# A hybrid decoder step: mLSTM heads in 128-token chunks with a carried state, stacked high and low parts, and alternating value products

## The reference

```python
ya = attend(q, k, v)                    # softmax attention; decoding rows read a paged key/value cache
# mLSTM of one head: b = cumsum(log f), i = input gate, m_t = running maximum
w_ts  = exp(b_t - b_s + i_s - m_t)      # s <= t
num_t = sum_s (q_t . k_s) w_ts v_s + a_t C q_t      # C: the state from before the chunk
den_t = sum_s (q_t . k_s) w_ts     + a_t n . q_t
h_t   = num_t / max(|den_t|, exp(-m_t))
C_new = a_end C + sum_s ws_s v_s k_s^T              # also an output, with n and m
u = sigmoid(ga) * (ya @ w_att) + sigmoid(gm) * (ym @ w_mlstm);  y = x + gate * (u @ w_out)
```

## Time and profile before

| | us |
|---|---|
| three runs | 715.68, 719.31, 721.13 |
| median | 719.31 |
| the profiled execution | 719.64 |
| its span, first to last instruction | 717.9 |
| mean granted TensorE clock, as a share of 2.4 GHz | 0.972 |

### The profile page before, as it was taken

The page is one execution under the profiler, slowest core; times in us unless marked ns, Lnnn a source line. Parts: engine busy times, 40 slices in busy tenths (PEclk is TensorE's granted clock), DMA queues, the critical chain, the costliest instruction groups (busy, mean ns, idle before and its releaser), DMA issues.

```text
span 717.9 us, 14725 instructions
## 1 busy us (share of the span) xinstructions
PE 680.0 (95%) x5000; PEld 605.8 (84%) x5000; DVE 472.7 (66%) x483; ACT 333.5 (46%) x725; POOL 430.0 (60%) x286
## 2 busy tenths in 40 slices
PE   1899999999999799999999999999999999999996
PEld 0477788888789668999999999998999999999974
DVE  0626578898989974995697686775384358433435
ACT  5546746456381336464464534632422225333643
POOL 4203565485686318698679688771775556666510
PEclk9889999999999889999999999999999999999999
DMA  8968459888898868377867667766776355833202
GB/s 316 345 201 266 148 160 281 250 264 271 238 295 251 264 208 246 105 235 212 232 207 228 186 189 229 231 208 170 187 193 179 93 178 148 266 89 93 83 30 89
DMA packets 156904, 144.72 MB, mean 202 GB/s; under 512 B 7547, under 2 KB 115152, under 8 KB 156852
## 3 DMA queue, kind: packets, MB, share of 16 engines
q1 hardware_dynamic: 142984, 137.15, 63.5%
q10 hardware_dynamic: 13876, 7.02, 3.2%
HBM read 135.10 MB, written 9.11 MB: 201 GB/s over the span
## 4 chain that ended last, share of the span: by engine, by line
PE 63%; issue 10%; POOL 10%; DVE 5%; SPq 5%; DMA 4%; ACT 2%; ACTq 0%; POOLq 0%; DVEq 0%
PE ps L554 46%; POOL sb_arenaA L1553 4%; POOL sb_wL L1509 4%; PE ps L984 3%; PE ps L814 2%; DMA sb_arenaA<-in_w_ada 2%; PE ps L586 1%; POOL sb_arenaA L1587 1%; SPq L395 1%; PE ps L924 1%; DVE sb_arenaB L1973 1%; PE ps L775 1%; DVE sb_arenaA L1968 1%; SPq L396 1%; PE ps L569 1%
## 5 line engine op out<-in xcount | busy, mean ns | idle before, releaser
L1509 POOL TENSOR_TENSOR sb_wL<-sb_wraw,sb_wH 128x512 fp32r<-128x512 f32 (+1 forms) x168 | 216.3, 1304 | 191.1 <-ACT sb_wH L1014 175.0
L554 PE MATMUL ps<-sb_hH,sb_wH 128*128 128x260 f32 x1152 | 241.9, 292 | 3.7 <-POOL sb_wL L1509 3.7
L554 PE MATMUL ps<-sb_hH,sb_wL 128*128 128x260 f32 x1152 | 235.1, 286 | 0.0
L554 PE MATMUL ps<-sb_hL,sb_wH 128*128 128x260 f32 x1152 | 234.8, 286 | 0.0
L554 PEld LDWEIGHTS ps<-sb_hH,sb_wH 128*128 128x128 f32 x1152 | 181.6, 193 | 19.1 <-issue 13.6
L1014 ACT ACTIVATE sb_wH<-sb_wraw 128x512 fp32r<-128x512 f32 (+1 forms) x168 | 99.2, 612 | 188.0 <-PE ps L554 145.4
L554 PEld LDWEIGHTS ps<-sb_hL,sb_wH 128*128 128x128 f32 x1152 | 181.2, 192 | 0.0
L554 PEld LDWEIGHTS ps<-sb_hH,sb_wL 128*128 128x128 f32 x1152 | 180.8, 192 | 0.0
L1587 POOL TENSOR_TENSOR sb_arenaA<-sb_arenaA 128x2048 f32<-128x2048 f32 x28 | 101.6, 3630 | 1.5 <-DMA sb_arenaA<-in_cache_v 1.5
L1553 POOL TENSOR_TENSOR sb_arenaA<-sb_arenaA 128x1024 f32<-128x1024 f32 x22 | 59.9, 2745 | 33.6 <-DMA sb_arenaA<-in_cache_k 33.6
L1829 DVE TENSOR_REDUCE sb_arenaA<-sb_arenaA 128x2048 f32 (+1 forms) x32 | 72.9, 2284 | 3.6 <-DVE sb_arenaA L1825 2.0
(11 more groups left out here) (385 smaller groups left out, 952.3 us busy)
## 6 DMA issues: line engine op xcount, KB each, us to landing
sb_wraw<-in_w_in SPq DMA_DIRECT2D x64, 512.0 KB, 5.3
sb_arenaA<-in_cache_k SPq DMA_DIRECT2D x128, 256.0 KB, 3.2
sb_arenaA<-in_cache_v SPq DMA_DIRECT2D x128, 256.0 KB, 3.1
sb_arenaA<-in_w_ada SPq DMA_DIRECT2D x6, 2048.0 KB, 12.2
sb_arenaB<-in_state_C SPq DMA_DIRECT2D x8, 512.0 KB, 3.9
sb_wraw<-in_w_mlstm SPq DMA_DIRECT2D x8, 512.0 KB, 4.9
sb_wraw<-in_w_out SPq DMA_DIRECT2D x8, 512.0 KB, 3.8
sb_arenaB<-in_x_prompt SPq DMA_DIRECT2D x1, 2048.0 KB
```

The lines of the kernel that those rows point to most:

```text
L554: last = mm(ps[:, 2 * s + a, 0:HALF], w[:, s, k, :], x[:, k, a * HALF:(a + 1) * HALF], start=(k == 0 and w is wH and x is xH), stop=(k == ...
L1509: tt(wL[:, j % 2, part], wraw[:, j % 4, part], wH[:, j % 2, part].bitcast(F32), ALU.subtract)\
```

## The change

1. **Chunks of 128 tokens in the mLSTM.** Only the four diagonal blocks of scores are made (4 matmuls of 128 columns). `kw` is scaled to the end of its own block, by `wa`, computed once. Four matmuls `kw x v1` give each block's own state; DVE chains them to the states after each block (`Cs`: one copy and three fused multiply-adds of 257 columns). The outputs are 4 matmuls for the diagonal and 3 for queries times the carried state; the queries are decayed first (`qd`: three exponentials on ACT, one product on DVE). The final state is the last `Cs`, turned by 3 transposes in place of 12 matmuls.
2. **Order in a head.** The key transposes stand right behind the scores. Both value transposes follow at once, in two banks. Tile n+4 stands before the state matmuls and tile n+5 between them and the outputs. In head 0 there is no tile there, and tile 0 of head 1 moves ahead of its closing transposes. On DVE `kw` moves ahead of `value_pair(6, h-1)`, and the chain of `Cs` stands behind it.
3. **Stacked high and low parts.** For `query_copy`, `key_query` and `spread_max` the high part lies in the lower rows and the low part from row 32 on, so one matmul over 36 or 40 rows does what two did (`spread_max` was fp32 and is now fp32r). The constants for it are built once on POOL, the small subtractions are on DVE.
4. **Alternating value products.** `pv` now does both heads of a round, alternating head 0 and head 1, once for each round. It stands where `pv(1)` stood, in the next round; `pv(0)` at the end of a round is gone. The turned weights `pT` get a buffer for each head.

```diff
-            def pv(e):
+            def pv():
                 for k in range(TT):
-                    last = mm(ps[DH * e:DH * e + DH, 7, k * P:T], vN[:, k, DH * e:DH * e + DH], pT[:, k, k * P:T],
-                              start=(k == 0), stop=(k == TT - 1))
+                    for e in range(2):
+                        last = mm(ps[DH * e:DH * e + DH, 7, k * P:T], vN[:, k, DH * e:DH * e + DH], pT[e][k],
+                                  start=(k == 0), stop=(k == TT - 1))
...
-                mm(ps[:, bank, :], selc[:, e, :], qsr[:, 0:AW], start=True, stop=False)
-                mm(ps[:, bank, :], selc[:, e, :], qsr[:, AW:2 * AW], start=False, stop=True).then_inc(qbc_mm, 1)
+                mm(ps[:, bank, :], selc[:, e, :], qsr, start=True, stop=True).then_inc(qbc_mm, 1)
...
                 if before:
-                    pv(1).then_inc(pv_done, 1)
+                    pe.wait_ge(qbc_rdy, 2 * t)
+                    pv().then_inc(pv_done, 1)
...
-                pe.wait_ge(qbc_rdy, 2 * t + 2)
-                pv(0)
...
-                mm(ps[:, 7, :], selm, MR[:, :], start=True, stop=True).then_inc(mb_mm, 1)
+                pe.wait_ge(mr_lo, 1)
+                mm(ps[:, 7, :], selm, MRr, start=True, stop=True).then_inc(mb_mm, 1)
...
-                for k, b, c in ((0, 4, 0), (1, 5, 0), (3, 5, 384), (2, 6, 0)):
-                    if first and b == 6:
-                        pe.wait_ge(mod_rdy, 5)
-                    last = mm(ps[:, b, c:c + T - k * P], qkc[:, 1, k * P:(k + 1) * P], qkc[:, 0, k * P:T],
-                              start=True, stop=True)
+                for k in range(TT):
+                    tok = slice(k * P, (k + 1) * P)
+                    last = mm(ps[:, 4, tok], qkc[:, 1, tok], qkc[:, 0, tok], start=True, stop=True)
                 last.then_inc(st_mm, 1)
...
+                else:
+                    ztile(0, n + 4, hH, hL)
                 pe.wait_ge(vt_ev, 2 * h + 2)
                 pe.wait_ge(v_one, 1)
...
-                for q in (0, 1, 3, 2):
-                    if q == 2:
-                        pe.wait_ge(kw_rdy, h + 1)
-                    for k in range(q + 1):
-                        last = mm(ps[:, 4 + q, 0:MV + 1], wt[:, k, (q - k) * P:(q - k + 1) * P], v1[:, k, :],
-                                  start=(k == 0), stop=(k == q))
+                pe.wait_ge(mpt_rdy, h + 1)
+                pe.wait_ge(kw_rdy, h + 1)
+                for k in range(TT):
+                    if first and k == 3:
+                        pe.wait_ge(mx_read, 2)
+                    last = mm(ps[:, 4 + k, 0:MV + 1], kw[:, k, :], v1[:, k, :], start=True, stop=True)
+                last.then_inc(k_mm, 1)
+                if not first:
+                    ztile(1, n + 5, hH, hL)
+                pe.wait_ge(cs_rdy, h + 1)
+                for q in range(TT):
+                    last = mm(ps[:, 4 + q, 0:MV + 1], wt[:, q, :], v1[:, q, :], start=True, stop=(q == 0))
+                    if q > 0:
+                        last = mm(ps[:, 4 + q, 0:MV + 1], qd[:, (q - 1) * P:q * P], Cs[:, q - 1, :], start=False, stop=True)
                 last.then_inc(pv_mm, 1)
                 if not first:
                     ztile(2, n + 6, hH, hL)
                 ztile(3, n + 7, hH, hL, pages_of=None if first else h)
+                if first:
+                    ztile(0, n + 8, hH, hL)
                 pe.wait_ge(hn_ev, 2 * h + 3)
...
-                    for part in range(2):
-                        first = (2 * part + a) * AW
-                        last = mm(ps[:, 4 + 2 * e + a, :], selg[:, e, :], kqr[:, first:first + AW],
-                                  start=(part == 0), stop=(part == 1))
+                    last = mm(ps[:, 4 + 2 * e + a, :], selg[:, e, :], kqr[:, a * AW:(a + 1) * AW], start=True, stop=True)
...
-                if first:
-                    choice_sums()
-                else:
+                if not first:
                     value_pair(4, h - 1, h == 1)
...
+                dve.wait_ge(kt_mm, h + 1)
+                dve.wait_ge(g_act, 3)
+                v.scalar_tensor_tensor(kw, ps[:, 6, :].rearrange("p (j n) -> p j n", j=TT), KSCALE,
+                                       wa[:, 0:TT, h:h + 1].broadcast_to([P, TT, P]), ALU.mult, ALU.mult).then_inc(kw_rdy, 1)
                 if first:
+                    choice_sums()
                     choice_total()
                 else:
                     value_pair(6, h - 1, h == 1)
...
+                dve.wait_ge(k_mm, h + 1)
+                chain(v.tensor_copy(Cs[:, 0, :], ps[:, 4, 0:MV + 1]))
+                for k in range(1, TT):
+                    last = v.scalar_tensor_tensor(Cs[:, k, :], Cs[:, k - 1, :], wa[:, TT + k - 1, h:h + 1],
+                                                  ps[:, 4 + k, 0:MV + 1], ALU.mult, ALU.add)
```

More of the change, by code:

```diff
@@ L211, in decoder_step @@
         prA = work(2 * TT * T, "p (e j n) -> p e j n", e=2, j=TT)
-        pT = work(TT * T, "p (j n) -> p j n", j=TT)
+        pT = [[work(T - k * P) for k in range(TT)] for _ in range(2)]
         used[0] = 0
@@ L729, in attention @@
                     for j in range(TT):
-                        last = tr(ps[:, 7, MH * j:MH * j + MH], MR[:, j * P:(j + 1) * P], ident[0:MH, 0:MH])
-                    last.then_inc(g_pe, 1)
+                        last = tr(ps[:, 7, MH * j:MH * j + MH], MR[0:MH, j * P:(j + 1) * P], ident[0:MH, 0:MH])
+                    mm(ps[:, 7, TT * MH:2 * TT * MH], ones[0:MH, :], ends, start=True, stop=True).then_inc(g_pe, 1)
                     ztile(3, n + 3, hH, hL, parts=(0,))
@@ L873, in _ @@
             mlstm(0, True)
[L874 to L875 removed]
+            mlstm(1, False, True)
+            with pe.Fori(0, MH - 2) as h:
+                mlstm(h + 2, False)
             ztile(0, T_GATE, hH, hL)
@@ L1146, in turned @@
                 for k, b, c in ((0, 4, 0), (1, 5, 0), (3, 5, 384), (2, 6, 0)):
-                    last = f(pT[:, k, k * P:T], ps[:, b, c:c + T - k * P], ACT.Copy)
+                    last = f(pT[e][k], ps[:, b, c:c + T - k * P], ACT.Copy)
                     if b == 4:
@@ L1295, in mlstm @@
                     act.wait_ge(vt_mm, 2 * h + u + 1)
-                    f(v1[:, :, u * P:(u + 1) * P], ps[:, 7, :].rearrange("p (j n) -> p j n", j=TT), ACT.Copy)\
+                    f(v1[:, :, u * P:(u + 1) * P], ps[:, 7 - 2 * u, :].rearrange("p (j n) -> p j n", j=TT), ACT.Copy)\
                         .then_inc(vt_ev, 1)
-                    if first:
-                        if u == 1:
-                            high(0, n + 8, quad + 2)
-                            leave(0, n + 6, gz[:, 0, :], ACT.Silu, chunk(gzS, 2 * h))
-                    else:
+                if first:
+                    high(0, n + 8, quad + 2)
+                    leave(0, n + 6, gz[:, 0, :], ACT.Silu, chunk(gzS, 2 * h))
+                else:
+                    for u in range(2):
                         high(2 + u, n + 6 + u, quad + 1)
@@ L1337, in _ @@
             with act.Fori(0, MH - 1) as h:
-                chain.loop(h, 1)
                 mlstm(h + 1, False)
-            chain.end(MH - 1)
             act.dma_start(O["conv_s"][0, :, 0:2, :], I["state_conv"][0, :, 1:3, :]).then_inc(st_misc, 16)
@@ L1998, in samples_joined @@
                     .then_inc(sam_dve, 1)
-                tt(cvS[:, :, :], cvS[:, :, :], cvP[:, :, :], ALU.add).then_inc(sam_dve, 1)
+                v.memset(cvS2, 0.0)
+                chain(tt(cvS[:, :, :], cvS[:, :, :], cvP[:, :, :], ALU.add))
+                dve.sem_inc(sam_dve, 1)
             def mlstm(h, first):
@@ L2019, in mlstm @@
                     value_pair(6, h - 1, h == 1)
-                dve.wait_ge(kt_mm, h + 1)
-                dve.wait_ge(wsc_rdy, h + 1)
-                v.scalar_tensor_tensor(kw, ps[:, 6, :].rearrange("p (j n) -> p j n", j=TT), KSCALE, over(wsc[:, :], P),
-                                       ALU.mult, ALU.mult)\
-                    .then_inc(kw_rdy, 1)
+                dve.wait_ge(k_mm, h + 1)
+                chain(v.tensor_copy(Cs[:, 0, :], ps[:, 4, 0:MV + 1]))
+                for k in range(1, TT):
+                    last = v.scalar_tensor_tensor(Cs[:, k, :], Cs[:, k - 1, :], wa[:, TT + k - 1, h:h + 1],
+                                                  ps[:, 4 + k, 0:MV + 1], ALU.mult, ALU.add)
+                    if k < TT - 1:
+                        chain(last)
+                last.then_inc(cs_rdy, 1)
                 if first:
```

169 lines of the change are left out of this document (93 added, 76 removed).

## The result

The changed kernel takes 739.25 us (median of 4 runs, 733.3 to 742.74) beside 720.22 for the kernel before: ratio 1.0278, 95% interval 1.0218 to 1.0338, so 2.8% slower. The forecast was slower, 728.0; the time lies above its range (716 to 734). The profiled execution took 742.74, span 741.0, against 719.64 and 717.9.

The account below looks back on a forecast made before the run. PE and a level loop through POOL and DVE's pair sum bound a head at 60.7 us. Attention -2.0, head 0 +1.3, heads +5.7, low clock +8.0, `key_query` -4.3 gave +8.7 on 719.64, as median 728.0; range 716 to 734.

Parts of the forecast that it names:

- The loop of a head: Heads 1 to 3: PE waits 4.1 us for `Cs` behind DVE's pair sum; period 62.4 for 60.7.
- The rival that PE stays the bound: PE's outputs in a head: chain of `Cs` hidden, PE's saving counts, 702.3 us; chance 0.13.
- Four waits of 2 to 4 us ... I take 2.0 each: Low PE clock behind one new wait in each of four heads: +8.0 us, ends 0 and 9.2.
- Head 0 ... together +1.3: Head 0: 4.6 us of new PE waits against -3.3 of PE work; +1.3, between -1 and +5.
- 8 x -0.54 = -4.3: `key_query`: each of eight calls takes 0.58 in place of 1.12 us; -4.3 (0 to -4.5).
- Attention -2.0: Attention: PE's saving of one `pv` and half of `query_copy` in a round, partly seen; -2.0 us (0 to -6).
- Head 0's last tile, forecast +1.8: Ahead of head 1, one tile now stands before head 0's closing transposes: +1.8 us, between 0 and +5.8.
- the 1.0 of the output gate: Between outputs and next convolution: the pair sum's 1.0 us wait for DVE's output gate goes, twice -1.0.
- the -2.35 behind the last outputs: Behind the last head's outputs: 2.35 us shorter, a term of the sum for heads 1 to 3.

Follow-up runs that it names:

- x2_fill_wait: Changed kernel with 20 unused PE matmuls in front of the wait for `Cs` in heads 1 to 3: 732.60 us, ratio 1.0211.
- x1_cs_first: Changed kernel with DVE making the chain of `Cs` ahead of the second pair sum in heads 1 to 3: 715.43 us, ratio 0.9957.
- the second profile: The profile of c1_changed_again, the changed kernel run once more with no edit: 738.42 us.
- x5_fill_all: As x2_fill_wait, plus in head 0 24 matmuls ahead of the wait for the choice sum and 8 ahead of `Cs`: 727.22 us, ratio 1.0123.
- c1_changed_again: Changed kernel run once more with no edit: 738.42 us, ratio 1.0265.
- z1_rest_alone: Kernel before with parts 3 and 4 of the change alone, without the chunks and with `spread_max` in fp32: 715.41 us, ratio 0.9952.
- y1_order_dve: Changed kernel, DVE reordered: `Cs` before the second pair sum (heads 1 to 3), choice sum first (head 0), `kw` ahead of `qd`: 707.33 us, ratio 0.9852.
- The twelve starts: Starts of head 0's convolution in twelve profiles of the changed kernel and its edits: 241.9 to 246.2, mean 244.1.

## Why the prediction was right and where it was wrong

The direction and the mechanism in the heads were right: PE waits for `Cs` behind the pair sum, and the clock falls behind that wait. The time was forecast 11 us too low. The steps that failed are the sizes of three terms of the sum: the low clock of a head (2.0 of the miss), head 0 (5.1) and `key_query` (3.8).

- **The loop of a head: right.** Pair sum at +20.7 (forecast 20.8), `Cs` at +31.3 (31.75), its chain 1.97 (2.2), outputs to next convolution 27.6 (27.6). With the clock held up (x2_fill_wait) outputs end at +34.7 (34.8) and the period is 62.4 (62.4). The rival that PE stays the bound was wrong for this order of DVE; x1_cs_first shows that it is right for the other one, in which `Cs` no longer waits for the pair sum.
- **"Four waits of 2 to 4 us ... I take 2.0 each": mis-sized.** The low clock behind a wait of 5.25 to 5.55 cost 2.65 in each of heads 1 to 3 (as much behind the 3.46 of head 1 in the second profile), since nearly all outputs ran at half clock; the price was sized on waits of 1.7 and 3.7. That is 2.0 of the miss. That the low clock comes from idling is shown by filling the wait. The rule cited from the Trainium skill ("TensorE: Matmul & The Clock Gate", section "HAM oscillation — how this bites in real kernels"), that each burst behind a wait starts at half clock, held for the outputs of all four heads: their first four records took 2.08, at full clock 1.14.
- **"Head 0 ... together +1.3", plus 2.0 of clock: mis-sized, +8.4 measured.** PE waited 6.6 for the sum over the choice (5.1 in the second profile), and not 2.4: of this, 3.29 was `qd`, which I priced at 0.55. Nearly all of block states and outputs then ran at half clock, 4.7 by x5_fill_all and not 2.0. These two, 2.7 each, are about the whole miss of 5.1. In heads 1 to 3 `qd` was free, as forecast; its cover, DVE's wait for POOL, isn't there in head 0. `qd`, POOL's instruction beside it, and PE's clock in head 0:

```profile
274.57 3.29 DVE L2039 TENSOR_TENSOR sb_arenaB<-sb_arenaB 128x384 f32<-128x384 f32 x1
```
```profile
273.83 3.61 POOL L1599 TENSOR_TENSOR sb_arenaA<-sb_arenaA 128x2048 f32<-128x2048 f32 x1
```
```profile
279.00:282.00 3.00, 1.49 (x5) 0.52 0.99 296
282.00:285.00 3.00, 2.70 (x7) 0.50 0.69 190
285.00:288.00 3.00, 1.23 (x3) 0.50 0.00 0
288.00:291.00 3.00, 3.00 (x8) 0.50 0.02 5
```

- **"8 x -0.54 = -4.3": -0.5 measured.** A call saves 0.45 (12.4 from call to call, not 12.8; the two matmuls take 0.73, not 0.58), some 3.6 in eight. The rest is given back behind the first call: 15.4 to the second one and not 12.4, 3.0 us lost. The first call and the clock behind it, in c1_changed_again:

```profile
528.34 1.09 PE L936 MATMUL ps<-sb_kqr 40*128 40x512 f32 x2 [1.59 <-DVE sb_kqr L2108]
```
```profile
528.30:531.30 3.00, 2.96 (x11) 0.52 1.17 299
531.30:534.30 3.00, 3.00 (x16) 0.50 1.12 275
534.30:537.30 3.00, 3.00 (x23) 0.84 0.04 11
```

  The clock is half there, behind a wait of 1.59 for DVE's low part (before: 0.51, with the clock at 1.00 behind it). That is the step that failed here: the forecast had a low clock only in the heads. z1_rest_alone has the same 15.4, behind a wait of 0.48; y1_order_dve has 13.9, behind 0.66. Why the clock falls at this place stays open.
- **Attention -2.0: neither shown nor refuted.** The twelve starts lie 1.5 below the one of before in the mean, with a scatter of 4 us.
- **The small terms.** Head 0's last tile, forecast +1.8, was +1.6; the 1.0 of the output gate was 1.0; the -2.35 behind the last outputs was -1.5, with the longer wait for DVE's low part in it (+1.1).

## What to carry to other kernels

Where a change makes one engine wait for a chain on another, look first at what stands ahead of that chain in the other's order: here an 8.5 us sum that itself waited for a third engine, and swapping the two turned +2.8% into -0.4%, with two more moves of that kind -1.5%. Price an idle wait of TensorE twice, once for itself and once for the low clock on what follows; here that was 5.3 and 2.6 us a head, and the second could be had back by useless matmuls in the wait. A saving on the busiest engine counts only after the loops that are level with it have been shortened too.

## What the runs showed of the hardware

A DVE instruction of 384 columns with both operands in SBUF took 0.54 to 3.29 us, and ended 0.41 to 0.44 behind the end of the POOL instruction that ran when it started, in two forms (plain product and fused). The weights product just before it, with one operand in PSUM, took 0.67 to 0.69 in every head, though POOL was at work then too. The Trainium skill ("SBUF — State Buffer", section "Who interferes with whom") says that a DVE instruction with two SBUF inputs and a POOL instruction that reads SBUF hold one shared port in turn; these rows agree with it, and the forecast had left this out.

Low clock followed waits of 5.25, 6.6 and 1.59 us here, and in z1_rest_alone one of 0.48, where the kernel before had 0.51 and no low clock. In head 1 of the changed kernel a wait of 2.76 for ACT left the granted clock at 1.00; one of 3.40 at the same place in c1_changed_again had 0.68 behind it. So the length of one wait doesn't tell whether the clock falls, and the runs leave open what decides it.

Two value products of 64 partitions took 2.38 when alternating, as much as one alone in the kernel before (2.37), and 3.93 in turn, not twice 2.38.
